# Prompt attention on one Trainium2 core: the order of query units in heads 1 to 3

## The reference

```
s = einsum('bqhc,bkc->bhqk', ql, ckv) + einsum('bqhr,bkr->bhqk', qp, kpe)
s = where(kpos <= qpos, s * MLA_SCALE, -inf)
p = softmax(s, axis=-1)
o = einsum('bhqk,bkc->bqhc', p, ckv)
```

## Time and profile before

| | |
|---|---|
| median of 3 runs | 2355.26 us (2346.83 to 2361.37) |
| the profiled execution | 2346.8 us, span 2345.0 us |
| PE busy | 2138.1 us (91% of the span), 20401 matmuls |
| DVE busy | 1298.9 us (55%) |
| ACT busy | 655.2 us (28%) |
| GpSimd busy | 216.0 us (9%) |
| mean granted TensorE clock | 0.958 of full speed |

### The profile page before, as it was taken

One profiled execution on the slowest core, in us unless ns is written; L12 is line 12 of the kernel. 1 busy time (PEld: TensorE's weight loads), 2 busy tenths in 40 slices (PEclk: granted clock), 3 DMA queues, 4 the chain that ended last, 5 costly groups with the idle time before them and its releaser, 6 DMA issues. The chain is left out here.

```text
span 2345.0 us, 48464 instructions
## 1 busy us (share of the span) xinstructions
PE 2138.1 (91%) x20401; PEld 1793.8 (76%) x20401; DVE 1298.9 (55%) x2838; ACT 655.2 (28%) x1471; POOL 216.0 (9%) x269
## 2 busy tenths in 40 slices
PE   7899999999999977598999899679799999699998
PEld 6899999987777764476777777558588888668886
DVE  6512444111111116499999999577477677554555
ACT  5311222000100001133343333244244444421110
POOL 0000000000000001122222222011402200000000
PEclk9999999999999995699999999889899999899999
DMA  7322332211121128699999999379999360254452
GB/s 247 110 71 80 98 98 91 82 64 64 63 81 63 46 65 286 262 372 356 370 378 371 359 370 375 132 265 351 260 185 157 59 109 14 105 196 151 149 164 81
DMA packets 183132, 422.02 MB, mean 180 GB/s; under 512 B 15056, under 2 KB 101360, under 8 KB 174728
## 3 DMA queue, kind: packets, MB, share of 16 engines
q0 software_dynamic: 45392, 236.13, 31.2%
q1 hardware_dynamic: 137536, 182.95, 23.3%
HBM read 325.54 MB, written 93.30 MB: 179 GB/s over the span
## 5 line engine op out<-in xcount | busy, mean ns | idle before, releaser
L607 PE MATMUL pj_ps<-pj_wh,pj_xh 128*128 128x256 f32 (+1 forms) x1152 | 326.3, 283 | 2.5 <-issue 2.5
L607 PE MATMUL pj_ps<-pj_wh,pj_xl 128*128 128x256 f32 (+1 forms) x1152 | 323.5, 281 | 0.0
L607 PE MATMUL pj_ps<-pj_wl,pj_xh 128*128 128x256 f32 (+1 forms) x1152 | 323.4, 281 | 0.0
L505 DVE TENSOR_SCALAR pj_stage<-pj_ps 128x256 f32<-128x256 f32 (+2 forms) x72 | 38.6, 536 | 481.3 <-PE pj_ps L605 314.2
L607 PEld LDWEIGHTS pj_ps<-pj_wh,pj_xh 128*128 128x128 f32 x1152 | 219.7, 191 | 10.4 <-issue 10.0
L1806 DVE STREAM_TRANSPOSE sa_turned<-sa_nat 128x2048 f32<-128x2048 f32 x96 | 220.0, 2292 | 11.5 <-DMA sa_kp<-cache_kpe,keep_index 11.5
L607 PEld LDWEIGHTS pj_ps<-pj_wl,pj_xh 128*128 128x128 f32 x1152 | 219.8, 191 | 0.0
L607 PEld LDWEIGHTS pj_ps<-pj_wh,pj_xl 128*128 128x128 f32 x1152 | 219.7, 191 | 0.0
L2030 PE MATMUL sa_ps_s<-sa_turned,keep_q 128*32 128x128 f32 x5120 | 182.9, 278 | 36.3 <-DVE sa_turned L1806 32.4
L605 PE MATMUL pj_ps<-pj_xh,pj_wh 128*128 128x512 f32 x512 | 202.7, 396 | 0.0
L605 PE MATMUL pj_ps<-pj_xl,pj_wh 128*128 128x512 f32 x512 | 201.0, 393 | 0.0
(11 more groups left out here) (410 smaller groups left out, 4209.2 us busy)
## 6 DMA issues: line engine op xcount, KB each, us to landing
pj_raw<-w_in POOLq DMA_DIRECT2D x16, 1024.0 KB, 6.4
s_zn<-pj_stage SPq DMA_DIRECT2D x64, 256.0 KB, 2.1
s_zt<-pj_stage SPq DMA_DIRECT2D x32, 512.0 KB, 2.6
rm_z<-s_zn SPq DMA_DIRECT2D x16, 768.0 KB
mg_gate<-s_zt SPq DMA_DIRECT2D x16, 768.0 KB, 6.5
mg_cat<-s_cat SPq DMA_DIRECT2D x16, 768.0 KB, 7.6
pn_x<-x_prompt SPq DMA_DIRECT2D x16, 512.0 KB, 5.8
s_k<-lp_st SPq DMA_DIRECT2D x16, 512.0 KB, 8.8
```

Source lines behind the costliest of these rows:

```text
L505: dve.tensor_scalar(stage_view(n, w_tile), ps[:, n % QUAD, 0:w_tile], factor(s), None, ALU.mult).then_inc(ev_dve, 1)
L607: mm = pe.matmul(ps[:, n % QUAD, 0:w], of[:, k, u * P:(u + 1) * P], wt[:, k, 0:w], **flags)
```

## The change

The units of head 0 keep their order 0, 1, 2, 3, 4, 5, 6, 7. The units of heads 1, 2 and 3 now come in the order 0, 7, 1, 6, 2, 5, 3, 4. Nothing else is edited; `order()`, the loads and the stores all follow the list `units`.

```diff
-        units = [(h, p) for h in range(HEADS) for p in range(PAIRS_Q)]
+        in_turn = range(PAIRS_Q)
+        by_turns = [p for n in range(PAIRS_Q // 2) for p in (n, PAIRS_Q - 1 - n)]
+        units = [(h, p) for h in range(HEADS) for p in (by_turns if h else in_turn)]
```

## The result

The changed kernel has a median of 2370.01 us over 6 runs (2366.68 to 2378.09), the kernel before one of 2354.51 (2346.83 to 2361.37, 6 runs). The medians lie 15.5 us apart. The ratio of the two, estimated over all runs, is 1.0078, with a 95% interval of 1.0061 to 1.0095: about 18 us slower, 14 to 22 by the interval. The profiled execution took 2366.68 us, with a span of 2364.9 us; before it was 2346.8, with a span of 2345.0.

What follows compares the result with a forecast made beforehand. PE paces the attention stage, busy 333 of 357 us. Waits of 29.7 us in and 12.4 out give 17.3, the clock +5: 22 us on 2346.8, 2369 profiled, median 2377; 8-of-10 range 2361 to 2391.

Steps and rivals of the forecast that it cites:

- waits removed: Heads 1 to 3: the 0.95 and 2.20 us waits at head starts and the unit-6 waits go, 12.4 us.
- unit 7 after 0, head 1: Start of head 1: PE idles 2.55 us before unit 7's turn, waiting for its two norms.
- the same, heads 2 and 3: Unit 7 after unit 0 there: PE waits 1.1 us for a low part; idle 3.6 us a head, 7.2 together.
- unit 6 after 1, each: Heads 1 to 3: PE idles 2.7 us before unit 6's turn for its norms, three times 8.1 us.
- unit 5 after 2, each: Heads 1 to 3: PE idles 1.4 us before unit 5's turn, three times 4.2; least certain term, 0 to 2.
- unit 4 after 3: End of heads 1 to 3: PE idles 2.4, 2.4 and 2.2 us before unit 4's turn, 7.0 us together.
- elsewhere: First steps of long units: exps after the scores delay a cast perhaps 0.2 us in unit 6; 0.6 us for all.
- falls of the clock behind the nine waits, net: Waits of 2.2 to 3.6 us: half drop the clock to 1.2 GHz at 1.54 us each, less one now: +5 us.
- Rival 1: Nine long waits: each drops the clock, 12.3 us on top of 17.3, 30 us slower, 2385; chance 0.17.
- Rival 2: Between short unit's low part and long unit's turn: DVE reaches norms early, added waits hidden, 12.4 us gained, 2343; chance 0.06.
- Rival 3: Unit 7's scores wait for a late load batch; 10 us a head gives 2405; chance 0.03.
- Rival 4: Added waits only about as large as those removed, within 10 us, if DVE gains time in two-step short units; chance 0.07.

Runs made afterwards that it cites:

- unit 7 filled: Changed kernel plus 16 matmuls with overwritten result ahead of unit 7's first turn in heads 1 to 3; one execution, 2369.97 us, stage 374.0 us.
- the early norms: Changed kernel with the long units' norms moved from the short unit into the long unit before it; median 2339.74 us, ratio 0.9931 to the kernel before.
- unit 6 filled: Changed kernel plus 16 matmuls with overwritten result ahead of unit 6's first turn in heads 1 to 3; one execution, 2365.61 us, stage 375.2 us.
- the run with one head: Only head 1 in the alternating order, heads 0, 2 and 3 ascending; 2357.92 us, ratio 1.0026 to the kernel before.
- the early norms alone: Kernel before, in ascending order, with norms placed in the long unit two units before their own; 2348.75 us, ratio 0.9969 to the kernel before.

## Why the prediction was right, point by point

It forecast 2377 us and 22 us more; the ratio says 18, the profiled stage 20.3. Its steps, forecast against the profile of the changed kernel:

| step | forecast | measured |
|---|---|---|
| waits removed | 12.4 | 12.4 (0.95, 2.20 and unit 6's, all gone in heads 1 to 3) |
| unit 7 after 0, head 1 | 2.55 | 2.54 |
| the same, heads 2 and 3 | 3.6 each | 0.80 + 2.28 each |
| unit 6 after 1, each | 2.7 | 2.68, 2.67, 2.68 |
| unit 5 after 2, each | 1.4 | 1.10, 1.10, 1.09 |
| unit 4 after 3 | 2.4, 2.4, 2.2 | 2.20, 2.23, 2.08 |
| elsewhere | 0.6 | none |
| waits, net | +17.3 | +14.3 |
| falls of the clock behind the nine waits, net | +5 (half of nine, less one) | +3.9 by what is left of the stage, +4.5 by busy time (four falls, less one) |
| the clock and the load in head 0 | 0 | +2.1 |
| loads behind head 0's start, end of stage | 0 | no wait for a load; the end not measured apart |

- **The mechanism** was that norms of long rows sit in DVE's queue where PE has almost nothing else. The experiment that moves them and the one that shortens them both show it. The reciprocal of unit 7's first norm began at T+1.51 in head 1, as read from the start of the old head 1:

```profile
1786.71 0.15 DVE L1244 RECIPROCAL la_soft<-la_soft 128x1 f32<-128x1 f32 x1
1786.90 1.22 DVE L1245 TENSOR_SCALAR la_row<-la_row,la_soft 128x1920 f32<-128x1920 f32 x1
...
1788.23 1.29 DVE L1245 TENSOR_SCALAR la_row<-la_row,la_soft 128x2048 f32<-128x2048 f32 x1
```

  with T = 1785.20, where PE began its last turn. The two norms and 0.35 end at 1789.58, the start of the turn.
- **The largest mis-sized term** is unit 7 in heads 2 and 3. The chain was right to 0.05 us: from the end of the scores, 1873.97, the values of group 4 began at S+4.42 (forecast 4.4), the turn at S+7.61 (7.66). What was off is PE's own work in between, 4.5 us and not 4.05. A turn of 3 blocks takes 0.49 us until it is drained, and I had counted only the 0.24 until the next start; so PE came to its first wait at S+3.62 and not S+3.3. The values after that wait took 0.91 us to their end and not 0.75, again the last matmul's drain. Where a wait follows, the whole length of the last matmuls counts. Unit 5's term has a slip of the same size: PE was ready at T+6.25 (forecast 6.05, where its own terms, 0.24 + 3.75 chunks at 1.2 + 1.41, add up to 6.15), and the turn came at T+7.35 (7.45). Unit 4's two points were each off by 0.1 (T+3.51, T+5.71).
- **The clock** was the term argued on the thinnest ground, one fall in three, and the sum was only near by a middle value. Falls came behind three waits for unit 7 and one for unit 4, never for unit 6. The run with unit 7 filled shows that unit 6 is not spared by its place.
- **Luck** is in the rest of the number. The waits were forecast 3.0 us too high, and 2.1 us in head 0, which no term stood for and which are not the change's, made up for most of it in the profile. The step from the profile to the median was 8.5 us in the forecast and 3.3 in the result (2366.68 to 2370.01).
- **Rival 1** (every long wait drops the clock) is wrong in this kernel, four falls of nine. The kernel in the section of "TensorE: Matmul & The Clock Gate" in the Trainium skill that the prediction named falls at every wait, but its waits are of 3 to 5 us by that page, longer than any of the nine. This case's traces show waits of 2.1 to 2.8 us followed by a fall or not.
- **Rival 2** (DVE gets to the norms early) did not happen, but its mechanism is exactly what the early norms turned into a gain.
- **Rival 3** is wrong: no wait for a load outside head 0's start. **Rival 4** too, since the interval of the difference (14 to 22 us) lies above its 10 us.

What stays open is why the low clock is hit at unit 7 in all three heads. The heads of the changed kernel are 92.0 and 92.06 us apart (1789.58, 1881.58, 1973.64), so what catches one may catch all three, and three falls in one profile are not three independent ones. Over all profiles, every unfilled wait for unit 7 had a fall behind it (3 of 3 in the changed kernel, 3 of 3 with unit 6 filled, 1 of 1 in the run with one head), and no unfilled wait for unit 6 that came after such a fall had one (0 of 3 and 0 of 1); after the filled unit 7 it was 3 of 3. Whether the one spares the other or timing does it, no run tells.

## What to carry to other kernels

When work of different sizes is interleaved to balance engines, look at what the *next* item must have finished, not at the sizes themselves: in a queue written out by hand a long item's preparation lands inside its short neighbour, where nothing covers it. Move the preparation one item further ahead first, and only then judge the order: here the same order went from 0.8% slower to 0.7% faster, and the early norms alone gave 0.3%.

A wait can be priced from one profile to within half a microsecond (here 0.01 to 0.5 off) if both chains are counted from a common instruction, the waited-for engine's and the waiting one's; the second has to include the drain of its last matmuls.

## What the runs showed of the hardware

A wait of PE of 2 to 2.8 us in a busy stretch lets the granted clock fall to 1.2 GHz in some cases and not in others: in heads 1 to 3 four of nine in the changed kernel, three of three in ascending order with early norms (2.42, 2.42, 2.19), one of three for 2.20 us in the kernel before. The same wait in head 0, 2.2 to 2.4 us, had a fall behind it in four of the nine profiles. The waits of 0.15 to 1.2 us in the heads of these kernels had none behind them. A fall cost 1.4 to 1.5 us, and filling the wait with matmuls whose result nobody reads gave it back. Filling one wait can move the fall to the next one, as at unit 6, so such a fill has to be judged by the whole stage.

The section "Part 4: PE-mode transpose" of "TensorE: Matmul & The Clock Gate" in the Trainium skill says that transposes don't count as activity for the clock as other matmuls do. Every long wait here has transposes behind it, some before it too. By that page such a wait would be longer for the clock than for the profile; no run here tells this apart.
